# Second attention: two steps' products with the values issued together, two scores in a row

## The reference

```python
def attend(qb):
    n = qb.shape[1]
    qb = qb.reshape(b, n, GQA_KV_HEADS, groups, GQA_HEAD_DIM)
    s = jnp.einsum('bqkgd,bskd->bkgqs', qb, k).astype(jnp.float32)
    p = jax.nn.softmax(s, axis=-1).astype(h.dtype)
    o = jnp.einsum('bkgqs,bskd->bqkgd', p, v)
    return o.reshape(b, n, GQA_Q_HEADS * GQA_HEAD_DIM)
```

## Time and profile before

| | us |
|---|---|
| median of 3 runs | 2755.56 |
| lowest and highest of them | 2755.27, 2759.28 |
| the profiled execution: its own time | 2760.81 |
| its span, from the first to the last instruction | 2758.9 |
| of the span, PE busy | 2688.9 |
| of the span, POOL, DVE, ACT busy | 1525.8, 1497.9, 943.2 |

### The profile page before, as it was taken

One profiled execution on the slowest core, in us unless ns is written; L12 is line 12 of the kernel. 1 busy time (PEld: TensorE's weight loads), 2 busy tenths in 40 slices (PEclk: granted clock), 3 DMA queues, 4 the chain that ended last, 5 costly groups with the idle time before them and its releaser, 6 DMA issues.

```text
span 2758.9 us, 39747 instructions
## 1 busy us (share of the span) xinstructions
PE 2688.9 (97%) x14623; PEld 2209.2 (80%) x14623; DVE 1497.9 (54%) x1962; ACT 943.2 (34%) x1630; POOL 1525.8 (55%) x1291
## 2 busy tenths in 40 slices
PE   8999999899999999999999899999998999999998
PEld 7888888699999999999777444454677888888886
DVE  4444444437444444445877866767356444545545
ACT  4343343324222222223321546554232222222224
POOL 5655655445655555556344657665445555655561
PEclk9999999999999999999999999999999999999999
DMA  7221221511111111111333000001211111112111
GB/s 225 64 60 57 61 71 46 206 43 54 57 50 49 46 46 46 46 49 54 103 82 62 19 1 16 16 1 62 89 46 54 46 57 49 49 54 59 51 54 65
DMA packets 200468, 163.06 MB, mean 59 GB/s; under 512 B 19816, under 2 KB 182032, under 8 KB 200352
## 3 DMA queue, kind: packets, MB, share of 16 engines
q1 hardware_dynamic: 193728, 139.83, 17.5%
q10 hardware_dynamic: 6624, 21.68, 2.0%
HBM read 131.70 MB, written 24.51 MB: 57 GB/s over the span
## 4 chain that ended last, share of the span: by engine, by line
PE 67%; issue 11%; POOL 11%; DVE 8%; DMA 1%; ACT 1%; SPq 1%; POOLq 0%; ACTq 0%; DVEq 0%
PE PS L984 17%; PE PS L916 11%; PE PS L1035 11%; PE PS L1180 9%; POOL wl L701 6%; PE PS L1454 4%; PE PS L1468 4%; POOL upraw L695 3%; PE PS L1231 2%; DVE nmx L2530 2%; PE PS L1267 2%; PE PS L1207 2%; DVE rcp L2559 2%; PE PS L1394 2%; POOL wraw L695 1%
## 5 line engine op out<-in xcount | busy, mean ns | idle before, releaser
L701 POOL TENSOR_TENSOR wl<-upraw,wh 128x512 fp32r<-128x512 f32 x212 | 285.3, 1348 | 271.6 <-ACT wh L1587 271.2
L675 POOL TENSOR_TENSOR wh<-wraw,ones 128x512 fp32r<-128x512 f32 x120 | 140.2, 1168 | 377.2 <-PE PS L916 200.1
L2081 DVE TENSOR_TENSOR h<-PS,h 128x1044 f32<-128x1044 f32 (+1 forms) x176 | 217.1, 1234 | 198.2 <-PE PS L1035 198.1
L1587 ACT ACTIVATE wh<-upraw 128x512 fp32r<-128x512 f32 x212 | 132.7, 630 | 502.3 <-POOL upraw L695 221.2
L1954 ACT ACTIVATE pf<-PS 128x512 f32<-128x512 f32 (+1 forms) x288 | 169.9, 594 | 167.1 <-PE PS L1454 165.9
L2530 DVE TENSOR_REDUCE nmx<-PS 128x1 fp32r<-128x1044 f32 x128 | 158.3, 1240 | 113.5 <-PE PS L1394 113.4
L678 POOL TENSOR_TENSOR wl<-wraw,wh 128x512 fp32r<-128x512 f32 x120 | 191.5, 1596 | 9.4
L701 POOL TENSOR_TENSOR wl<-wraw,wh 128x512 fp32r<-128x512 f32 x74 | 98.7, 1334 | 154.3 <-ACT wh L1587 154.3
L857 POOL TENSOR_TENSOR accp<-accp,pf 128x1024 f32<-128x1024 f32 x64 | 152.0, 2376 | 19.3 <-ACT pf L1954 18.4
L1817 ACT ACTIVATE pt<-PS 128x512 f32<-128x512 f32 x128 | 75.8, 593 | 243.6 <-PE PS L1231 237.0
L1468 PE MATMUL PS<-pf,vg 128*64 128x512 f32 x576 | 156.0, 621 | 0.0
(11 more groups left out here) (342 smaller groups left out, 7298.3 us busy)
## 6 DMA issues: line engine op xcount, KB each, us to landing
upraw<-in_ffn_w SPq DMA_DIRECT2D x166, 256.0 KB, 2.8
wraw<-in_ffn_w SPq DMA_DIRECT2D x98, 256.0 KB, 2.8
wraw<-in_a_w_qkv SPq DMA_DIRECT2D x48, 256.0 KB, 2.8
biasb<-bias_shifts SPq DMA_DIRECT2D x128, 72.0 KB, 2.5
h_spill<-h ACTq DMA_DIRECT2D x16, 522.0 KB, 5.0
h<-h_spill ACTq DMA_DIRECT2D x8, 522.0 KB, 7.5
h<-h_spill SPq DMA_DIRECT2D x8, 522.0 KB, 6.9
xt<-in_x SPq DMA_DIRECT2D x16, 256.0 KB, 6.9
```

What stands on the lines that cost most here:

```text
L701: nc.gpsimd.tensor_tensor(wlr[l][slot], rb[l][r], whr[l][slot].bitcast(F32), ALU.subtract).then_inc(s_wrd, 1)
L1587: nc.scalar.activation(whr[l][(o + 1) % ring], rb[l][r], ACT.Copy).then_inc(s_xhi, 1)
L2081: nc.vector.tensor_tensor(out_, x, y, op_).then_inc(sem_, 1)
```

## The change

In every step the two `scores` now follow each other, and then comes `tile_max`. The `p_v` are issued in odd steps alone, behind `tile_max`: `p_v(s - 3)`, then `p_sums`, `v_by_key` and `late_spread` where a step has them, then `p_v(s - 2)`, then `max_row`. In even steps there is no `p_v`. The last two `p_v` stay behind the loop. Nothing is computed differently and no other engine's program changes.

```diff
                 scores(s, 0)
-                if s >= LAG:
-                    p_v(s - LAG)
-                if kt == SUM_AT and n:
-                    p_sums(n - 1)
-                if kt == ROW_AT[0] + 1 and bp in V_AT and g + 1 < NG:
-                    pe.wait_ge(s_mset, 2 * n + 3)
-                    v_by_key(g + 1, V_AT.index(bp))
                 scores(s, 1)
...
                 if kt < BT and not last:
                     tile_max(n + 1, kt)
+                if s % 2 and s >= LAG + 1:
+                    p_v(s - LAG - 1)
+                if kt == SUM_AT and n:
+                    p_sums(n - 1)
+                if kt == ROW_AT[0] + 1 and bp in V_AT and g + 1 < NG:
+                    pe.wait_ge(s_mset, 2 * n + 3)
+                    v_by_key(g + 1, V_AT.index(bp))
                 if n < 4:
                     late_spread(n, kt)
+                if s % 2 and s >= LAG + 1:
+                    p_v(s - LAG)
                 if kt == ROW_AT[0] and not last:
```

## The result

The changed kernel takes **2767.3 us** (median of 7 runs), the one before, run beside it, 2758.9 (median of 7): ratio 1.0025, 95% interval 1.0015 to 1.0035. So it is slower, by 4 to 10 us (8.4 between the medians), a small difference but clear of the noise. The forecast was 14.6.

What follows compares the result with a forecast made beforehand. PE's order and waits were taken to bound the attention. Waits of 53.7 against 19.8 (+33.9) less 19.3 of saved form changes gave +14.6 us, from the median of 2755.6 to 2770.0; range 2760 to 2781.

Steps and rivals of the forecast that it cites:

- What bounds the attention: Order and spacing of PE's products set the attention's time: PE busy 405.5 of 416 us, DVE 285.
- The saving, 0.34 for each pair: Adjacent `p_v` in odd steps save changes of array form: 0.34 us a pair, 56 x 0.34 = 19.0.
- The wait for the reduction: In each pair the second maxima's product waits until 1.97 us behind the first: 37.0 in all against 16.9.
- The copy of the row of maxima: The next block's second `scores` waits for `set_max`: 0.4 to 0.5 for each of 15 blocks, 6.2 in all.
- The exponentials: An odd step's second `scores` waits for the even step's second exponential: some 0.1 us, up to 0.5; 10.5 against 2.9.
- the walk: PE, ACT, DVE and POOL carried in program order through 144 steps: waits 53.7 against 19.8, changes -19.3, sum +14.6 us.
- The hand sum: Two ordinary blocks: waits 5.1 and 1.1 against 2.6, less 9 - 1 savings of 0.34: about +1.0 to 1.5.
- some 4 more: Added us in the first four blocks, where `late_spread` and DVE's `scale_late` lie in the same steps.
- the forecast's own bounds of +12 and +17.5: The delay of a released wait, taken as 0.05 us: 0 gives +12.0, 0.10 gives +17.5.
- rival 2: Savings and waits cancel: hidden weight loads or unseen exponential waits take away 8 to 11: about +5, 2760; chance 0.13.
- (1), the changes of form decide: The reduction doesn't hold `tile_max` in odd steps, so savings stand almost alone: about -11, 2745; chance 0.07.
- (3), a falling clock: The 1.9 us waits in step 6 of 7 blocks lower PE's clock, 2.9 each: 20, so 2790; chance 0.06.

Runs made afterwards that it cites:

- experiments 1 and 2: DVE's maxima reduction reads 116 of 348 columns, exponentials scaled: in the order of before 2742.8 us (0.9932), in the order of after 2733.9 (0.9898).
- the second short kernel: The changed kernel's order with DVE's maxima reduction cut to 116 of 348 columns and exponentials scaled: 2733.9 us, ratio 0.9898.
- experiments 1, 2, 5 and 6: Orders of before and after: reduction cut to 116 columns (1, 2: 2742.8, 2733.9 us); output parts behind steps 2, 4, not 3, 4 (5, 6: 2753.2, 2760.5).

## Why the prediction was right, and where its size was off

**What bounds the attention: right.** PE's order and waits do, and DVE bounds nothing by its sum (228.5 of 340 us) but by the distance of two reductions.

**The saving, 0.34 for each pair: right.** In after two `p_v` take 1.87 where they took 2 x 1.01, and the two further terms are the same times as before. Take all gaps between the starts of PE's products in blocks 1 to 15, and put each kind (the same two products in a row) at the shortest seen in either trace: these sum to 18.5 us less in after, where the forecast had 19.3 saved in all 16 blocks. The forecast's 19.3, less what the exponentials and the copy took (16.7 against 2.9), left 5.5 of gain without the reduction's waits; experiments 1 and 2 found 9.2, since those two terms were smaller, as told below.

**The wait for the reduction: right in place and size.** The step of 1.97 is the measured 1.98, step 6 of odd blocks 1.84 against 1.9. All waits of maxima's products in blocks 1 to 15, counted as what these gaps are longer than the shortest, are 28.8 us and 5.3 of weight loads: 34.1. Before, the same count gives 15.1. The forecast's 37.0 and 16.9 hold block 0 too. The difference is 19.0 against 20.1; experiments 1 and 2 put it at 17.4, and the second short kernel still has 2 us more of these waits than the first. Block by block, an even one has 1.4 to 1.7 of them (forecast 1.64) and an odd one 3.2 to 3.4 (forecast 3.5). Even blocks of 24.4 to 25.1 and odd ones of 28.0 to 28.4 were forecast as about 25 and 28.6.

**The copy of the row of maxima: right in place, too large.** It was put at 0.4 to 0.5 for each block, 6.2 in all. In blocks 1 to 15 of after the second score's own gap is 2.8 us longer in sum, and with 15 weight loads of 0.11 that makes 4.5: 0.41 in blocks behind an even step 8, 0.21 behind the others. There `max_row` follows the pair of `p_v` and takes 0.50 rather than 0.40 itself, which is 0.10 of the difference; the other 0.10 was not looked into.

**The exponentials: right in place, and the term that was far too large.** The prediction had the second score of an odd step wait "some 0.1 us", and 10.5 in the sum against 2.9 before. By the starts such waits are about 3 us more than before in blocks 1 to 15, half of them in block 15, and at most pairs they come to nothing. Two things in the working as written are too large. First, it counts one 0.23 twice: the second matmul of a `scores` starts 0.23 behind the first and the exponential 0.44 behind that, so a lone exponential ends 0.23 + 0.44 + 0.60 = 1.27 behind the second `scores`, not 1.5. Second, in this order the exponential is not alone. Queued behind its neighbour, at 0.60 for each, it would end 1.40 behind, just when it is wanted. But two in a row take 1.09 together, as the row of 1762.86 shows, so it is done at 1763.95, 1.29 behind the second `scores` (1762.66) and 0.13 ahead of the score that wants its bank (1764.08). That score's weight load, let go at 1764.00, is just in time. The trace of before had such pairs in the last block. A row of a lone instruction is too dear for one that is queued behind its like.

How much of the 10.5 each of these made is open: of the walk only the sums are on record. The hand sum says where it must have stood: for two ordinary blocks it has 1.1 of waits other than at the maxima, of which 0.8 to 1.0 is the copied row, so nearly all of the 10.5 lay in the first four blocks and in block 15. The "some 4 more" of the first four blocks did not come: blocks 1, 2 and 3 changed by +2.2, -1.3 and +2.0, as ordinary ones do. (Block 0 can't be read from the trace of before; in the kernels of experiments 1, 2, 5 and 6 it is 0.8 to 1.0 longer in the order of after.)

**The sum.** In blocks 1 to 15 the waits and weight loads grew by 19.0 at the maxima, 4.5 at the copied row and about 3 at the exponentials, together +26.7; the rest of the gaps shrank by 18.5: +8.1. The hand sum was nearer to this than the walk. Its terms give 5.1 + 1.1 - 2.6 - 8 x 0.34 = +0.9 for two ordinary blocks (the text rounds it up to 1.0 to 1.5), and -1.2 + 2.2 = +1.0 was measured; with 7.5 such pairs and the 4 it makes 10.6, not 14.6.

**What was luck.** 2770.0 was forecast and 2767.3 measured, but before took 2758.9 beside it and not the 2755.6 from which the forecast counted; 3.3 us of the agreement are that. The change itself was +8.4, a little over half of +14.6, below the forecast's own bounds of +12 and +17.5, and nearer to rival 2's +5. The range held it because its lower end was taken from that rival.

**The rivals.** (1), the changes of form decide, needs the wait gone. Experiments 1 and 2 made that case, and there the change gains 8.9 us, where the rival had 11. (2), savings and waits nearly cancel, was wrong in its first half, since the weight loads do show (0.66 against 0.55 above). Its second half, exponentials that don't show, is in the main what happened. (3), a falling clock, did not occur: the granted clock was 1.00 from 1536 to 1956 us. The rule of the Trainium skill that a change of tiling mode drains TensorE (TensorEngine Tiling (Array Packing), Tiling Modes) agrees with the 9.2 us of experiments 1 and 2 in that changes of form cost; no run here tells a drain from the weight load that is not hidden behind a `p_v`. By that rule alone the sign would have been wrong.

## What to carry to other kernels

Before grouping work on the busiest engine, list what each instruction leaves as distance between two uses of one buffer: here a `p_v` was also the time that the reduction had, and taking it out of every other step put 1.40 us where 1.97 were needed. Distances count pair by pair; that the engine which must keep up is busy only two thirds of the time does not settle it. And look for long instructions queued behind two adjacent urgent ones on that engine: moving one part of the output by one step gave 7 us in the order of before, about as much as the change cost.

## What was not expected of the hardware

Two exponentials of 128 x 512 in a row take 1.09 us, and one alone 0.60, so the second costs 0.49. And a maxima's product that waits for the reduction loses its early weight load, which costs 0.11 beyond the wait, in the shortest waits seen (0.10 to 0.15 us) as in those of 1.7; in the order of after that is some 5 us in blocks 1 to 15.
